# Second attention's heads set between the projections around it, the masked quarter left out, and finer waits in the opening

## What is computed

```
# start: h = x + 0.5 * swiglu(rmsnorm(x, ffn1_norm), ffn1_w_gate_up, ffn1_w_down)
# last mixer (layer 1 of the second block):
kv = rms_norm(x, ln_kv) @ w_kv;  shared_k = rope(kv[:, :128]);  shared_v = kv[:, 128:]   # 2 kv heads of 64
h = rms_norm(x, ln_mix[1]);  proj = h @ swa_w_q                 # 768 columns of q, 256 of memory queries
q = rope(proj[:, :768])                                         # 12 heads of 64
# 12 masked heads: causal, window 128, in blocks of 128 queries, one sink logit a head
s = where(band, q k^T / 8, -inf);  m = max(max(s), sink);  p = exp(s - m);  p = p / (sum(p) + exp(sink - m))
# 4 memory heads: softmax(mem_q mem_k^T / 8) over 256 memory rows
x = x + concat(masked outputs, memory outputs) @ w_out[1]
```

## Time and profile before

| | us |
|---|---|
| median of 3 runs | 1700.3 (1697.75 to 1701.42) |
| profiled execution, device time | 1702.51 |
| its span, first to last instruction | 1700.7 |
| TensorE matmul busy | 1584.5 |
| GpSimd busy | 1166.0 |
| ScalarE busy | 807.3 |
| VectorE busy | 583.1 |
| mean granted TensorE clock | 0.962 of full |

### The profile page before, as it was taken

One profiled execution on the slowest core, in us unless ns is written; L12 is line 12 of the kernel. 1 busy time (PEld: TensorE's weight loads), 2 busy tenths in 40 slices (PEclk: granted clock), 3 DMA queues, 4 the chain that ended last, 5 costly groups with the idle time before them and its releaser, 6 DMA issues.

```text
span 1700.7 us, 21777 instructions
## 1 busy us (share of the span) xinstructions
PE 1584.5 (93%) x8746; PEld 1357.5 (80%) x8746; DVE 583.1 (34%) x1040; ACT 807.3 (47%) x1192; POOL 1166.0 (69%) x490
## 2 busy tenths in 40 slices
PE   4999999999978698999999999889999988899997
PEld 3888879999967577878878888877888876578886
DVE  4111018245449712331121586552113046521100
ACT  4444363466353435355454773135444353355443
POOL 4888868887756286478877872606887952078883
PEclk9999999999989898999999998989999987899998
DMA  6555645555545154355545542004555631055551
GB/s 210 173 192 192 204 167 185 187 184 194 164 140 175 54 178 137 102 198 183 189 161 193 192 155 78 1 25 136 195 176 198 195 123 55 25 174 182 189 197 51
DMA packets 71861, 259.80 MB, mean 153 GB/s; under 512 B 7984, under 2 KB 8784, under 8 KB 71504
## 3 DMA queue, kind: packets, MB, share of 16 engines
q1 hardware_dynamic: 68832, 249.59, 44.3%
q10 hardware_dynamic: 2928, 8.81, 1.5%
HBM read 257.29 MB, written 1.08 MB: 152 GB/s over the span
## 4 chain that ended last, share of the span: by engine, by line
PE 86%; DVE 7%; ACT 5%; issue 2%; DMA 0%; POOL 0%; ACTq 0%; DVEq 0%
PE bank L459 12%; PE bank L461 12%; PE bank L460 12%; PE bank L429 7%; PE bank L430 7%; PE bank L431 6%; PE bank L488 5%; PE bank L490 5%; PE bank L489 5%; PE bank L568 1%; ACT w_hi L1000 1%; PE bank L614 1%; PE bank L840 1%; PE bank L852 1%; PE bank L637 1%
## 5 line engine op out<-in xcount | busy, mean ns | idle before, releaser
L387 POOL TENSOR_TENSOR w_lo<-raw,w_hi 128x1024 fp32r<-128x1024 f32 x474 | 1143.1, 2433 | 464.6 <-ACT w_hi L1000 464.1
L1000 ACT ACTIVATE w_hi<-raw 128x1024 fp32r<-128x1024 f32 x474 | 489.1, 1057 | 467.1 <-PE bank L461 211.6
L459 PE MATMUL bank<-w_hi,u_hi 128*128 128x512 f32 x880 | 352.1, 400 | 31.5 <-POOL w_lo L387 20.0
L461 PE MATMUL bank<-w_hi,u_lo 128*128 128x512 f32 x880 | 346.2, 393 | 0.0
L460 PE MATMUL bank<-w_lo,u_hi 128*128 128x512 f32 x880 | 346.1, 393 | 0.0
L429 PE MATMUL bank<-u_hi,w_hi 128*128 128x256 f32 x880 | 252.8, 287 | 12.9 <-DVE u_lo L1584 6.4
L430 PE MATMUL bank<-u_lo,w_hi 128*128 128x256 f32 x880 | 250.6, 285 | 0.0
L431 PE MATMUL bank<-u_hi,w_lo 128*128 128x256 f32 x880 | 250.6, 285 | 0.0
L459 PEld LDWEIGHTS bank<-w_hi,u_hi 128*128 128x128 f32 x880 | 167.4, 190 | 68.3 <-issue 22.7
L461 PEld LDWEIGHTS bank<-w_hi,u_lo 128*128 128x128 f32 x880 | 167.3, 190 | 36.0
L460 PEld LDWEIGHTS bank<-w_lo,u_hi 128*128 128x128 f32 x880 | 167.6, 190 | 33.4
(11 more groups left out here) (354 smaller groups left out, 1871.3 us busy)
## 6 DMA issues: line engine op xcount, KB each, us to landing
raw<-in_w SPq DMA_DIRECT2D x474, 512.0 KB, 4.2
bc<-acs_scratch ACTq DMA_DIRECT2D x8, 512.0 KB, 5.8
mem_t<-in_mem ACTq DMA_DIRECT2D x2, 1024.0 KB, 7.7
xf<-in_x ACTq DMA_DIRECT2D x2, 512.0 KB, 8.3
out<-out_t SPq DMA_DIRECT2D x4, 256.0 KB, 2.8
lvl<-in_lvl ACTq DMA_DIRECT2D x1, 448.0 KB, 5.6
band<-in_band ACTq DMA_DIRECT2D x1, 256.0 KB, 5.2
tri<-in_tri ACTq DMA_DIRECT2D x1, 192.0 KB, 7.8
```

Source lines behind the costliest of these rows:

```text
L387: nc.gpsimd.tensor_tensor(w_lo[:, q % RAW, :], raw[:, q % RAW, :], w_hi[:, q % HI, :].bitcast(F32), ALU.subtract).then_inc(split_done, 1)
L459: mm(b[:], hi[:, kt, a], w_hi[:, q % HI:q % HI + 2, c], start=kt == 0, stop=False)
L461: m = mm(b[:], lo[:, kt, a], w_hi[:, q % HI:q % HI + 2, c], start=False, stop=kt == KT - 1)
L1000: fn(w_hi[:, q % HI, :], raw[:, q % RAW, :], ACT.Copy).then_inc(hi_made, 1)
```

## The change

In the weight stream, mq1 comes before q1. In the opening, par has a semaphore of its own, and the engines wait for ident, ones and tri only where they first need them; SyncE waits for the first half of x instead of the second; both first w_hi come after the fourth u_hi. In the last mixer:

- rotation: VectorE multiplies the row in PSUM with cosines and with sines into two SBUF tiles; TensorE adds them up as ident x first + rot x second (four fp32 products); VectorE copies the result to k2 or q2.
- scores take three banks of their own in turn; the q1 rows use two banks in turn, wo1's first column half these two.
- for masked heads, the first 128 queries meet only 128 keys in mask, scores, maximum, exponential, normalising, turning and output.
- normalising moves to ScalarE; one exponential of the sink for both halves.
- outputs go to h_hi and h_lo instead of u_hi and u_lo, which q1 still needs.
- TensorE's order: the heads' steps stand between half chunks of q1 and tiles of wo1. ScalarE's weight feeds stand between its exponentials.
- first_pair, which did wo0's first half in single tiles of the contraction, is moved up and used for wo1 too. kv_v is done by nat_piece, which issues the same products.

```
-    ("kv_v", 1, "nat"), ("kv_k", 1, "row"), ("q1", 3, "row"), ("mq1", 1, "row"), ("wo1", 4, "proj"),
+    ("kv_v", 1, "nat"), ("kv_k", 1, "row"), ("mq1", 1, "row"), ("q1", 3, "row"), ("wo1", 4, "proj"),
...
                 if q == 2:
-                    sp.wait_ge(W["loaded_x1"], 16)
+                    sp.wait_ge(W["loaded_x0"], 16)
...
-            load(ident[:], ident_in, "loaded_par")
+            load(ident[:], ident_in, "loaded_const")
...
-            act.wait_ge(W["loaded_par"], 64)
+            act.wait_ge(W["loaded_par"], 16)
...
-                if kt in (1, 3):
-                    feed(1 if kt == 1 else 2)
+                if kt == 3:
+                    feed(2)
...
```

TensorE, the new order and its new functions (scores, the score banks and the order of the units stand in the source in full):

```
+            row_stage("mq1", u_hi, u_lo)
+            rotate(0)
+            row_stage("q1", u_hi, u_lo, sub=(0, 1))
+            scores(0)
+            scores(1)
+            scores(2)
+            row_stage("q1", u_hi, u_lo, sub=(1, 1), halves=(0,))
+            rotate(1)
+            turns(0)
+            row_stage("q1", u_hi, u_lo, sub=(1, 1), halves=(1,))
+            turns(1)
+            turns(2)
+            row_stage("q1", u_hi, u_lo, sub=(2, 1), halves=(0,))
+            rotate(2)
+            heads_out(0)
+            turns(3)
+            turns(4)
+            heads_out(1)
+            row_stage("q1", u_hi, u_lo, sub=(2, 1), halves=(1,))
+            turns(5)
+            turns(6)
+            rotate(3)
+            heads_out(2)
+            turns(7)
+            turns(8)
+            heads_out(3)
+            turns(9)
+            turns(10)
+            heads_out(4)
+            pe.wait_ge(row_free, G0["q1"] + 3)
+            wo1_tiles(6, 7)
+            turns(11)
+            wo1_tiles(0)
+            turns(12)
+            heads_out(5)
+            wo1_tiles(1)
+            turns(13)
+            wo1_tiles(2)
+            turns(14)
+            heads_out(6)
+            wo1_tiles(3)
+            turns(15)
+            heads_out(7)
+            wo1_tiles(4, 5)
+            proj_stage("wo1", h_hi, h_lo, None, lambda: turn("ffn3", 0), pairs=(1,))
...
+            def rotate(n):
+                b = start_unit(att2_unit("R", n))
+                pe.wait_ge(W["rope_cs"], 2 * n + 2)
+                ...
+                for t in range(2):
+                    mm(b[:, t, :], ident[:], rtmp[0][:, t, :], start=t == 0, stop=False, skip_group_check=True)
+                    m = mm(b[:, t, :], rot[:], rtmp[1][:, t, :], start=False, stop=t == 1, skip_group_check=True)
+                m.then_inc(unit_done, 1)
...
+            def scores(i):
+                b = score_banks[i % 3]
+                if i >= 3:
+                    pe.wait_ge(W["at_exp"], h2 + i - 2)
+                ...
+                    for c in range(2):
+                        o, n = b[:, c, 0:P * (c + 1)], P * (c + 1)
+                        mm(o, ident_r[:], band_r[:, c, 0:n], start=True, stop=False)
+                        m = mm(o, q[:, c * P:c * P + P], k[:, 0:n], start=False, stop=True)
+                m.then_inc(W["at_score"], 1)
...
+            def probs_turn(i):
+                b = flat(start_unit(att2_unit("T", i)))
+                pe.wait_ge(W["at_p"], h2 + i + 1)
+                for c in range(2):
+                    for mc in range(2 if i < 4 or c else 1):
+                        o = 2 * P if i >= 4 and mc else mc * S + c * P
+                        m = nc.tensor.transpose(b[:, o:o + P], pr[i % 4][:, c, mc * P:mc * P + P], ident[:])
+                m.then_inc(unit_done, 1)
...
+            def heads_out(o):
+                b = start_unit(att2_unit("O", o))
+                pe.wait_ge(unit_free, att2_unit("T", 2 * o + 1) + 1)
+                ...
+                        p0 = P if h >= 4 and mc else 0
+                ...
+                        m = mm(b[64 * t:64 * t + 64, 0, p0:S], v_h, src, start=mc == 0, stop=mc == 1, skip_group_check=True)
+                m.then_inc(unit_done, 1)
...
+            def turns(i):
+                probs_turn(i)
+                if i + 3 < 16:
+                    scores(i + 3)
```

ScalarE and VectorE:

```
+            def normalise(i):
+                act.wait_ge(W["at_rec"], i + 1)
+                for c in range(2):
+                    p = pr[i % 4][:, c, 0:P if i >= 4 and c == 0 else S]
+                    m = fn(p, p, ACT.Identity, scale=stat(5, i)[:, c:c + 1])
+                m.then_inc(W["at_p"], 1)
...
+            after(P0["q1"] + 1)
+            for i in range(16):
+                act.wait_ge(W["at_max"], h2 + i + 1)
+                for c in range(2):
+                    n = P if i >= 4 and c == 0 else S
+                    m = fn(pr[i % 4][:, c, 0:n], score_banks[i % 3][:, c, 0:n], ACT.Exp, bias=stat(1, i)[:, c:c + 1], scale=0.125,
+                           accum_out=stat(2, i)[:, c:c + 1])
+                if i >= 4:
+                    m = fn(stat(3, i), stat(1, i), ACT.Exp, bias=col("sinks", i - 4))
+                m.then_inc(W["at_exp"], 1)
+                if i >= 4 and i % 2 == 0:
+                    out_hi(i // 2 - 2)
+                if i:
+                    normalise(i - 1)
+                if i in (1, 3, 4, 7):
+                    after(P0["q1"] + {1: 2, 3: 3, 4: 4, 7: 5}[i])
+            normalise(15)
+            out_hi(6)
+            after(P0["wo1"] + 1)
+            out_hi(7)
             after(P0["wo1"] + 3)
...
+            def rope(n):
+                dve.wait_ge(piece_done, done("kv_k") if n == 0 else done("q1", n))
+                ...
+                v.tensor_tensor(rtmp[0][:], b[:], cs[:, 0:1, :].to_broadcast([P, 2, S]), ALU.mult).then_inc(W["rope_cs"], 1)
+                v.tensor_tensor(rtmp[1][:], b[:], cs[:, 1:2, :].to_broadcast([P, 2, S]), ALU.mult).then_inc(W["rope_cs"], 1)
+                dve.wait_ge(W["rope_cs"], 2 * n + 2)
+                dve.sem_inc(row_free, 1)
...
+            for i in range(16):
+                reciprocal(i)
+                if i >= 4 and i % 2 == 0:
+                    out_lo(i // 2 - 2)
+                if i == 0:
+                    turned_out(1)
+                else:
+                    probs_out(i - 1)
+                if i in (3, 7):
+                    turned_out(2 if i == 3 else 3)
+                if i + 2 < 16:
+                    row_max(i + 2)
+                if i in (2, 6):
+                    rope(2 if i == 2 else 3)
```

More of the change, by code:

```diff
@@ L316, in proj_bank, with row_bank, att2_unit @@
         def proj_bank(name, s, p):
+            if name == "wo1":
+                return bank[(G0["mq1"] + s + p * (3 - 2 * s)) % 4]
             return bank[4 + 2 * s + p] if name == "mix" else bank[[FB[0], FB[2], FB[1], TB][2 * s + p]]
+        def row_bank(r):
+            if r >= G0["mq1"]:
+                return bank[(G0["mq1"] + (r - G0["mq1"]) % 2) % 4] if r < G0["q1"] + 3 else bank[r % 4]
+            return bank[r % 4]
+        score_banks = [bank[G0["kv_v"] % 4], bank[G0["kv_k"] % 4], bank[4]]
+        def att2_unit(what, i):
+            return U0["att2"] + ATT2.index((what, i))
         def turned(name, s, kt):
@@ L526, in proj_stage, with first_pair @@
                             halfway()
+            def first_pair(name, hi, lo, kts, ready):
+                for kt in kts:
+                    q = P0[name] + 2 * (kt // 4)
+                    if kt in (6, 0):
+                        pe.wait_ge(split_done, q + 2)
+                    c = slice(kt % 4 * S, kt % 4 * S + S)
+                    for s in range(2):
+                        ready(s, kt)
+                        b, a = proj_bank(name, s, 0)[:], slice(s * P, s * P + P)
+                        mm(b, hi[:, kt, a], w_hi[:, q % HI:q % HI + 2, c], start=kt == 6, stop=False)
+                        mm(b, hi[:, kt, a], w_lo[:, q % RAW:q % RAW + 2, c], start=False, stop=False)
+                        m = mm(b, lo[:, kt, a], w_hi[:, q % HI:q % HI + 2, c], start=False, stop=kt == 5)
+                        if kt == 5 and s == 0:
+                            m.then_inc(acc_part, 1)
+                    if kt in (3, 5):
+                        m.then_inc(piece_done, 2)
             def turn(name, s, src=x):
@@ L890, in _ @@
             next(memory)
[L892 to L908, removed]
             pe.wait_ge(row_free, G0["gz"] + 3)
@@ L926, in _, with kv_ready @@
             turn("kv", 0, xn)
[L927 to L938, removed]
-                        mm(b[:, s, :], h_hi[:, kt, a], w_lo[:, q % RAW, c], start=False, stop=False, skip_group_check=True)
-                        m = mm(b[:, s, :], h_lo[:, kt, a], w_hi[:, q % HI, c], start=False, stop=kt == KT - 1 and s == 1, skip_group_check=True)
-                m.then_inc(piece_done, 1)
+            def kv_ready(s):
+                pe.wait_ge(n_lo, 16 * SPL["kv"] + 8 * s + 8)
@@ L955, in _ @@
-            for j in range(3):
-                row_stage("q1", u_hi, u_lo, sub=(j, 1))
-                rotate(j)
-            row_stage("mq1", u_hi, u_lo)
-            rotate(3)
-            pe.wait_ge(row_free, G0["mq1"] + 1)
+            h2 = HEAD0["att2"]
```

(15 more changed lines are left out.)

121 lines of the change are left out of this document (82 added, 39 removed).

## The result

After: 1690.3 us median (1688.16 to 1691.59, 4 runs); before, beside it, 1700.8 (1697.75 to 1701.42, 4 runs). The ratio is 0.9941, 95% interval 0.9923 to 0.9958: 10.5 us faster, where 21.6 had been forecast. The profiled execution took 1691.59, its span 1689.8.

The account below looks back on a forecast made before the run. TensorE, busy for 93% of the span, was taken to bound the kernel. From 1702.5 us, -15.0 (attention) and -6.6 (opening) gave 1680.9, and with the median 2.2 below the profiled execution, 1679; range 1667 to 1692.

Parts of the forecast that it names:

- the attention's term: Second attention, first q1 matmul to end of wo1: 96.6 us against 111.63, so -15.0 us.
- the first rival: Second attention's heads: small VectorE operations blocked 10 us, not 2.5, or 15 us clock drop costing 7.5; 1686.5, chance 0.18.
- My own sign of being wrong: Second attention: TensorE's idle before turns sums to over 20 us, or new low clock stretches between 1400 and 1480.
- Work and stalls: Second attention: TensorE's new order, part by part with stalls, takes 94.1 us; with 2.5 for small VectorE operations, 96.6.
- 85.9 are work: Second attention: the part of TensorE's 94.1 us without stalls; it sets the low end of the range, 1667.
- The small operations: Second attention: VectorE's negated maximum and sum with the sink, delayed by POOL; 2.5 us taken, between nothing and 12.
- the 12 us: Second attention: upper bound for delayed small VectorE operations, one blocked 2.45 us for each of five weight pieces; time 1688.
- Opening: Kernel's start: first matmul at 16.85 instead of 19.44, hid's start near 34.8 instead of 39.70, no low clock; -6.6 us.
- Sum: Whole kernel: 1702.5 - 15.0 - 6.6 = 1680.9 us for the profiled execution, 1679 for the median.
- Rival 2: Opening: its loads come no earlier, only the attention gains; 1685.5 us, chance 0.08.
- Rival 3: Second attention: ScalarE's queue makes each head's chain run alone, 5.4 us a head; slower, 1727.7 us, chance 0.08.
- Rival 4: Second attention: opening of rotation and mq1 only moves the idle time before wo1; within 2 us, 1699, chance 0.04.

Follow-up runs that it names:

- e5: Kernel before with 27 useless 512-column products on TensorE in the second attention's waits: 1687.5 us, ratio 0.9933.
- e1: Kernel before with the opening's edits alone: 1697.0 us against 1699.8, ratio 0.998.
- e7: Kernel after with the opening's edits taken back, leaving the attention's change: 1691.7 us against 1699.3, ratio 0.996.
- e2: Kernel after with the negated maximum and the sum with the sink each split into two one-column VectorE operations: 1688.8 us, ratio 0.9937.
- e4: Kernel after with TensorE's order changed: wo1's tiles start after turn 7, one between most turns of heads 8 to 11: 1686.0 us, ratio 0.9918.
- e10: Kernel after with only the third of e6's five fillers, 10 transposes ahead of rotation 3: 1685.7 us, ratio 0.9918.
- e11: Kernel after with only the first two of e6's five fillers, 14 transposes ahead of turns 3 and 4: 1689.8 us, ratio 0.9942.
- e3: Kernel after with 22 useless 512-column products on TensorE at five places where it idled: 1680.7 us, ratio 0.9889.
- e6: Kernel after with 44 transposes of 128 columns as filler at the same five places as e3: 1680.1 us, ratio 0.9886.
- e12: e6 with the masked quarter of heads 4 to 15 computed again: 1684.4 us, ratio 0.9911.
- e8: Kernel after with e2's split operations, e4's spread tiles, e3's filler at its first three places and an early table load: 1677.7 us, ratio 0.9875.

## Why the prediction was wrong

Stretch A side by side, with the time in it that TensorE was granted 1.2 GHz:

| kernel | stretch A | at 1.2 GHz |
|---|---|---|
| before / with filler (e5) | 111.63 / 100.54 | 30.7 / 0 |
| opening alone (e1) | 110.96 | 27.3 |
| after / attention alone (e7) | 108.18 / 108.15 | 30.7 / 30.7 |
| e2 split / e4 spread | 104.48 / 102.12 | 23.9 / 13.6 |
| e10 third filler / e11 first two | 104.41 / 104.54 | 20.5 / 20.5 |
| e3, e6 five fillers | 95.92, 96.01 | 0 |
| e12 with the quarter | 101.81 | 0 |
| e8 best | 95.04 | 0 |

Against its like with a held clock, a microsecond at 1.2 GHz costs 0.36 (before against e5: 11.1 / 30.7) to 0.45 (e4 against e6: 6.1 / 13.6); after's 30.7 cost 12.2.

- **The step that failed** is the clock in the attention's term: that TensorE would work heads 7 to 10 "at clock 1.00", in 6.0 a pair, "the pace of now". My reason against the first rival was that "with TensorE at 90% the clock stood at 1.00 for 23.93 us, and no stall of mine is over 1.4". That window's busy share was an average of two things: up to 1463.0 TensorE hardly waited, and behind it came waits of 0.28 and 1.74; the clock fell at 1466.6, in the next wait, of 1.21. Before, the row up to 1463.28, and the first two waits in the timeline:

```profile
1442.39:1463.28 20.89, 20.54 (x105) 11.60 (x104) 17.71 (x54) 10.15 (x44) 0.00 (x0) 1.00 0.00 0
```

```profile
1463.28 0.63 PE L626 MATMUL bank<-ident,pr 128*128 128x128 f32 x4 [0.28 <-DVE pr L1615]
1465.65 0.63 PE L626 MATMUL bank<-ident,pr 128*128 128x128 f32 x4 [1.74 <-DVE pr L1615]
```

The stretch at a full clock was no evidence that the clock survives waits of 1.3, for up to its last 3 us it had none. So I took out of the sum before's clock cost (11.1), put in none for after, and after paid 12.2. Of the -15.0, the work that is left out was 4.6 (100.54 to 95.92), and the other 10.4 was clock that never came back. My own sign of being wrong, new stretches at a low clock between 1400 and 1480, came true. The Trainium skill (TensorE: Matmul & The Clock Gate, section A second HAM failure mode: psum-queue depth-cycling) tells of a kernel whose short pauses between groups of products let the clock swing; I had not weighed it. These traces agree: after's clock fell at 1421.2 behind waits of 1.38 and 0.58, and at 1431.5 in one of 1.31.
- **Work and stalls** were right, once the clock is held: 95.92 and 96.01 against 96.6. After's waits sum to 7.1, where I had 7.7; most were where I had put them (normalising before turns, 0.5 to 1.4), but the 1.31 before rotation 3 I hadn't foreseen. The "85.9 are work" should be 86.4, the 94.1 less the 7.7 of stalls, which moves only the low end of my range, by 0.5.
- **The small operations**: five of the sixteen negated maxima met a GpSimd operation and were blocked: L2221 took 3.5 us for four and L2223 6.0 for twelve, where a free one takes 0.17 and 0.23, so some 6.0 too much on VectorE, and little of it on the path. In e2 the wait before rotation 3 shrank from 1.31 to 0.48 and one of 0.52 vanished: about 1.3 us directly, half of my 2.5. The blocking was real, but it met 5 operations and not 28, and the 12 us didn't come.
- **Opening**: forecast -6.6; hid's turn came 5.5 earlier (38.68 against 44.15), with no low clock behind it, as said. Most of what it fell short by is the table load, which I had hidden before x, and which in after began only when x was in (9.37): 1.28 us, shown by e8. e8's first product came within 0.04 of the forecast.
- **Sum**: 1702.5 - 3.45 - 5.5 = 1693.6, and after's profiled execution took 1691.6. The other 2 us lie in code that both share: e7 and before issue the same work until kv_v, and kv_v begins 2.9 earlier in e7 (1366.44 against 1369.31). One thing that differs between the two traces is the clock: from 200 to 230 it was 0.94 before and 1.00 in e7, from 1025 to 1075 it was 0.83 and 0.90. Where the clock falls varies from execution to execution.
- **Rival 1** named the mechanism (a clock drop in the bare middle) and had it at 15 us and 7.5; it was 30.7, of which 27.3 on end, and 12.2. Rivals 2, 3 and 4 fell: the opening gained, no head's chain runs alone, and the merge isn't void.

What stays open: which waits bring a fall and which don't (turn 7's 1.27 in e10 and in e8), and why e2's median is only 1.5 us under after's, where its stretch A gained 3.7; its six runs span 8.7 us.

## What to carry to other kernels

Where TensorE waits for 1 to 2 us every few us, as here, price the clock before the waits: read the granted clock where waits of that size stand, not where there are none, and never from a busy share that averages both. Before reordering work to close such gaps, fill them with products that nobody reads, in a free bank: it is a few lines, it shows what the clock costs, and here it was worth as much as the whole change (1687.5 against 1690.3). Where the waits themselves set the pace, as around kv_v, filler gains little.

## What had not been expected of the hardware

- After's clock fell at 1431.5, in a wait of 1.31, and stayed at 1.2 GHz for 27.30 us with only two more waits, of 1.27, in them; TensorE was busy for 23.95 of the 27.30.
- A VectorE scalar operation on 128x2 elements in SBUF took 2.24 us beside a GpSimd operation of 2.37; on 128x1 two took 0.33 beside one of 2.35, and a reciprocal on 128x2 took 0.15.
- The activation table's load takes 1.28 us. In after it began only when x had landed, at 9.37; with a one-column activation on par ahead of the wait for x it began at 4.05, before that activation's own input was in (5.75). Why it waited in one kernel and not in the other is open.
